# Two small edits in a fused two-layer transformer kernel: relative-bias rows from one 8-column matmul spread by the DMA, and indexer scores of an even and an odd head side by side

## The reference

```python
rel = jax.nn.relu(jnp.einsum("bqhd,bsd->bqhs", qib, k_idx_f))
score = jnp.einsum("bqhs,bqh->bqs", rel, wb) * idx_scale
score = jnp.where(admissible[None], score, -jnp.inf)
_, sel = lax.top_k(score, topk)
```

```python
dist = q_pos[:, None] - k_pos[None, :]
bias = jnp.transpose(rel_bias[rel_bucket(dist)], (2, 0, 1))
logits = jnp.einsum('bqhcd,bkhcd->bhcqk', q_blk, k) * scale + bias[None, :, None]
```

## Time and profile before

| | |
|---|---|
| median of 3 runs | 2699.56 us (2699.01 to 2699.8) |
| profiled execution, its own time | 2699.8 us |
| span of its profile | 2698.0 us |
| PE busy | 2584.3 us (96%) |
| DVE busy | 1684.5 us (62%) |
| ACT busy | 1286.2 us (48%) |
| granted clock of PE, mean | 0.988 |

### The profile page before, as it was taken

How to read it: one execution, slowest core, us unless ns; L and a number is a source line. 1 busy time by engine, 2 the same in 40 slices (tenths; PEclk the granted TensorE clock), 3 DMA queues, 4 the chain that set the end, 5 groups by cost and what they waited for, 6 DMA issues and landing times.

```text
span 2698.0 us, 28994 instructions
## 1 busy us (share of the span) xinstructions
PE 2584.3 (96%) x11660; PEld 2111.5 (78%) x11660; DVE 1684.5 (62%) x1914; ACT 1286.2 (48%) x1797; POOL 3.4 (0%) x10
## 2 busy tenths in 40 slices
PE   4999989999989999999999899999999999999998
PEld 3777767877868888888888787778788888888886
DVE  6899788988875555555555544666554454445455
ACT  4535666755454444444444454544454444444443
POOL 0000000000000000000000000000000000000000
PEclk9999999999989999999999999999999999999999
DMA  9888445777855556665554554345455555555553
GB/s 352 326 332 324 157 156 197 270 281 278 342 222 203 218 204 234 241 242 212 209 205 176 180 186 158 141 156 187 172 177 195 187 195 197 188 194 194 188 187 125
DMA packets 80566, 579.29 MB, mean 215 GB/s; under 512 B 8964, under 2 KB 8964, under 8 KB 10544
## 3 DMA queue, kind: packets, MB, share of 16 engines
q1 hardware_dynamic: 78480, 564.82, 57.8%
q10 hardware_dynamic: 1440, 9.81, 0.9%
q0 software_dynamic: 512, 2.81, 0.3%
HBM read 573.73 MB, written 3.67 MB: 214 GB/s over the span
## 4 chain that ended last, share of the span: by engine, by line
PE 76%; DVE 7%; ACT 3%; issue 1%; DMA 0%; ACTq 0%; DVEq 0%; SPq 0%
PE bank L640 72%; DVE wlo L1459 2%; PE bank L604 1%; ACT whi L965 1%; DVE raw L1469 1%; DVE X L1454 1%; DVE cv L1664 1%; ACT PR L965 0%; DVE SS L1454 0%; DVE cv L1454 0%; PE bank L752 0%; PE bank L800 0%; ACT SS L1335 0%; DMA raw<-in_w_in 0%; PE bank L885 0%
## 5 line engine op out<-in xcount | busy, mean ns | idle before, releaser
L1459 DVE TENSOR_TENSOR wlo<-raw,whi 128x1024 fp32r<-128x1024 f32 x882 | 1077.3, 1224 | 957.1 <-ACT whi L965 953.4
L965 ACT ACTIVATE whi<-raw 128x1024 fp32r<-128x1024 f32 x882 | 932.3, 1059 | 1289.2 <-PE bank L640 1169.2
L640 PE MATMUL bank<-whi,HTh 128*128 128x512 f32 x2560 | 706.2, 398 | 8.8 <-ACT HTh L965 5.8
L640 PE MATMUL bank<-wlo,HTh 128*128 128x512 f32 x2560 | 687.6, 391 | 3.5 <-DVE wlo L1459 3.5
L640 PE MATMUL bank<-whi,HTl 128*128 128x512 f32 x2560 | 689.2, 391 | 0.5 <-DVE HTl L1775 0.5
L640 PEld LDWEIGHTS bank<-wlo,HTh 128*128 128x128 f32 x2560 | 481.6, 188 | 106.4 <-DVE wlo L1459 4.8
L640 PEld LDWEIGHTS bank<-whi,HTl 128*128 128x128 f32 x2560 | 483.5, 189 | 103.7 <-DVE HTl L1775 1.0
L640 PEld LDWEIGHTS bank<-whi,HTh 128*128 128x128 f32 x2560 | 472.5, 189 | 113.9 <-issue 15.6
L1469 DVE CUSTOM_DVE_ANT_0 raw<-raw,GT,VECS 128x2048 f32<-128x2048 f32 x96 | 225.0, 2347 | 0.2 <-DMA raw<-in_w_ada 0.2
L640 PE MATMUL bank<-whi,ACTh 128*128 128x512 f32 x704 | 191.6, 394 | 0.0
L640 PE MATMUL bank<-wlo,ACTh 128*128 128x512 f32 x704 | 190.0, 392 | 0.0
(11 more groups left out here) (217 smaller groups left out, 1235.5 us busy)
## 6 DMA issues: line engine op xcount, KB each, us to landing
raw<-in_w_in SPq DMA_DIRECT2D x128, 1024.0 KB, 4.9
raw<-in_w_ada SPq DMA_DIRECT2D x96, 1024.0 KB, 6.5
raw<-in_w_gate SPq DMA_DIRECT2D x88, 1024.0 KB, 4.8
raw<-in_w_up SPq DMA_DIRECT2D x88, 1024.0 KB, 4.8
raw<-in_w_down SPq DMA_DIRECT2D x88, 1024.0 KB, 4.8
raw<-in_w_o SPq DMA_DIRECT2D x16, 1024.0 KB, 7.0
raw<-in_w_out SPq DMA_DIRECT2D x16, 1024.0 KB, 4.8
raw<-in_w_attn_out SPq DMA_DIRECT2D x8, 1024.0 KB, 4.8
```

The source lines that it names most:

```text
L640: i = e.matmul(bank[2 * ch.st + t][:, :], (xl if ps == 1 else xh)[:, k, tk(t)], (lo if ps == 2 else hi)[:, j * 512:j * 512 + 512], start=c ...
L965: return e.activation(dst, src, ACT.Copy, scale=scale)
L1459: e.tensor_tensor(lo, src, r32(hi), S_).then_inc(lo_done, 1)
```

## The change

Bias rows: one matmul with the eight heads as its eight columns gives all rows at once, in eight partitions; ACT copies them once; the scratch write repeats each row 128 times. The table `relb` is no longer repeated on the host. Scores: each slot takes an even and an odd head, which lie in the two halves of the array, for both halves of the tokens; the two heads go to banks 6 and 7, which are now one tensor `both`, and one ReLU reads 384 columns of each. The 384 are 256 of t = 1 and 128 of t = 0. Counters for the two halves become one.

```diff
-    RB = at("RB", 41984, [8, 128])
-    RD = at("RD", 50176, [8, 384])
+    RB = at("RB", 41984, [8])
+    RD = at("RD", 50176, [384])
...
+    rel = [at(f"rel{i}", 75776 + 4096 * i, [2, 512]) for i in range(2)]
...
-    bank = [nc.alloc_psum_tensor(f"bank{i}", [128, 512], f32) for i in range(8)]
+    bank = [nc.alloc_psum_tensor(f"bank{i}", [128, 512], f32) for i in range(6)]
+    both = nc.alloc_psum_tensor("bank67", [128, 2, 512], f32)
+    bank += [both[:, 0, :], both[:, 1, :]]
...
-            for h in R(8):
-                if h == 0:
-                    w.wait_ge(*xt_act(14))
-                else:
-                    w.wait_ge(*rb_act(h - 1))
-                e.matmul(bank[5][:, 0:384], RB[0:33, h, :], OH[0:33, :], start=True, stop=True).then_inc(*rb_pe.one(h))
-                yield 1
+            w.wait_ge(*xt_act(14))
+            e.matmul(bank[5][0:8, 0:384], RB[0:33, :], OH[0:33, :], start=True, stop=True).then_inc(*rb_pe.one("rows"))
+            yield 1
...
             for hp in R(8):
-                half = hp % 2
                 if hp:
-                    w.wait_ge(*sel_act[t](hp - 1))
-                for r in R(2):
-                    h = 4 * (hp // 2) + 2 * r + half
-                    i = e.matmul(b[:, r * 256:r * 256 + nk], qiT[64 * half:64 * half + 64, h // 2, tk(t)],
-                                 kiT[64 * half:64 * half + 64, 0:nk], start=True, stop=True)
-                i.then_inc(*sel_pe[t].one(hp))
+                    w.wait_ge(*sel_act(hp - 1))
+                for t in (1, 0):
+                    nk = 128 * (t + 1)
+                    for r in R(2):
+                        i = e.matmul(bank[6 + r][:, 256 - 256 * t:256 - 256 * t + nk], qiT[64 * r:64 * r + 64, hp, tk(t)],
+                                     kiT[64 * r:64 * r + 64, 0:nk], start=True, stop=True)
+                i.then_inc(*sel_pe.one(hp))
                 yield 1
...
-            for h in R(8):
-                w.wait_ge(*rb_pe(h))
-                copy(RD[:, h, :], bank[5][:, 0:384]).then_inc(*rb_act.one(h))
-                yield 1
+            w.wait_ge(*rb_pe("rows"))
+            copy(RD[0:8, :], bank[5][0:8, 0:384]).then_inc(*rb_act.one("rows"))
+            yield 1
...
-                e.activation(tri(sg[:, :], 2)[:, :, 0:nk], tri(b[:, :], 2)[:, :, 0:nk], ACT.Relu,
-                             scale=1.0 / 32).then_inc(*sel_act[t].one(hp))
+                e.activation(rel[hp % 2][:, :, 0:384], both[:, :, 0:384], ACT.Relu, scale=1.0 / 32).then_inc(
+                    *sel_act.one(hp))
...
                 for r in R(2):
-                    h = 4 * (hp // 2) + 2 * r + hp % 2
+                    sg = rel[hp % 2][:, r, 256 - 256 * t:256 - 256 * t + nk]
+                    h = 2 * hp + r
...
-        e.dma_start(A["scratch"], RD[:, :, :]).then_inc(scr_in, 16)
+        e.dma_start(A["scratch"].rearrange("p h i -> h p i"), RD[0:8, :].unsqueeze(1).to_broadcast([8, 128, 384])).then_inc(
+            scr_in, 16)
...
-    out["relb"] = np.broadcast_to(relb[:, :, None], (33, 8, 128))
+    out["relb"] = relb
```

More of the change, by code:

```diff
@@ L369, in build @@
     fh_act = steps("fh_act", list(R(16)))
-    rb_pe = steps("rb_pe", list(R(8)))
-    rb_act = steps("rb_act", list(R(8)))
+    rb_pe = steps("rb_pe", ["rows"])
+    rb_act = steps("rb_act", ["rows"])
     u_act = steps("u_act", [(j, t) for j in R(2) for t in R(2)])
@@ L377, in build @@
     two_dve = steps("two_dve", [0, 1])
-    sel_pe = [steps(f"sel{t}_pe", list(R(8))) for t in R(2)]
-    sel_act = [steps(f"sel{t}_act", list(R(8))) for t in R(2)]
+    sel_pe = steps("sel_pe", list(R(8)))
+    sel_act = steps("sel_act", list(R(8)))
     sel_dve = [steps(f"sel{t}_dve", [("s", hp, r) for hp in R(8) for r in R(2)] + ["outside"]
@@ L676, in bias_rows @@
             w.wait_ge(rb_in, 32)
-            for h in R(8):
-                if h == 0:
-                    w.wait_ge(*xt_act(14))
-                else:
-                    w.wait_ge(*rb_act(h - 1))
-                e.matmul(bank[5][:, 0:384], RB[0:33, h, :], OH[0:33, :], start=True, stop=True).then_inc(*rb_pe.one(h))
-                yield 1
+            w.wait_ge(*xt_act(14))
+            e.matmul(bank[5][0:8, 0:384], RB[0:33, :], OH[0:33, :], start=True, stop=True).then_inc(*rb_pe.one("rows"))
+            yield 1
         def t_job(n):
-            w.wait_ge(*rb_act(7))
+            w.wait_ge(*rb_act("rows"))
             if n:
@@ L700, in t_job, with select @@
             yield 1
-        def select(t):
-            nk = 128 * (t + 1)
-            b = bank[6 + (t == 0)]
+        def select():
             w.wait_ge(*tj_act("qi4", 1))
@@ L721, in attend @@
             bs = [bank[7]] if t == 0 else [bank[6], bank[5]]
-            w.wait_ge(*sel_act[t](7))
+            w.wait_ge(*sel_act(7))
             w.wait_ge(*tj_act("k4", 1))
@@ L936, in tensor @@
             lane.begin(TJ_SLOT[n], t_job(n))
+        lane.begin(SEL0, select())
         for t in R(2):
-            lane.begin(SEL0, select(t))
             lane.begin(ATT0 + 5 * (t == 0), attend(t))
@@ L1127, in t_job, with select @@
             yield 1
-        def select(t):
-            nk = 128 * (t + 1)
-            b = bank[6 + (t == 0)]
+        def select():
             for hp in R(8):
-                sg = stg[t + 2 * (hp % 2)]
-                w.wait_ge(*sel_pe[t](hp))
+                w.wait_ge(*sel_pe(hp))
                 if hp >= 2:
-                    w.wait_ge(*sel_dve[t]("s", hp - 2, 1))
-                e.activation(tri(sg[:, :], 2)[:, :, 0:nk], tri(b[:, :], 2)[:, :, 0:nk], ACT.Relu,
-                             scale=1.0 / 32).then_inc(*sel_act[t].one(hp))
+                    for t in R(2):
+                        w.wait_ge(*sel_dve[t]("s", hp - 2, 1))
+                e.activation(rel[hp % 2][:, :, 0:384], both[:, :, 0:384], ACT.Relu, scale=1.0 / 32).then_inc(
+                    *sel_act.one(hp))
                 yield 1
@@ L1168, in conv_products @@
             w.wait_ge(*cv_dve("pad"))
-            w.wait_ge(*rb_pe(7))
+            w.wait_ge(*rb_pe("rows"))
             w.wait_ge(*pro_dve("lam1"))
@@ L1588, in select @@
             for hp in R(8):
-                sg = stg[t + 2 * (hp % 2)]
-                w.wait_ge(*sel_act[t](hp))
+                w.wait_ge(*sel_act(hp))
                 for r in R(2):
-                    h = 4 * (hp // 2) + 2 * r + hp % 2
+                    sg = rel[hp % 2][:, r, 256 - 256 * t:256 - 256 * t + nk]
+                    h = 2 * hp + r
                     if prev is None:
-                        m = e.tensor_scalar(sc, sg[:, 0:nk], WI[:, t, 0:1], None, M_)
+                        m = e.tensor_scalar(sc, sg, WI[:, t, 0:1], None, M_)
                     else:
                         w.wait_ge(*sd(*prev))
-                        m = stt(sc, sg[:, r * 256:r * 256 + nk], WI[:, t, h:h + 1], sc, M_, A_)
+                        m = stt(sc, sg, WI[:, t, h:h + 1], sc, M_, A_)
                     m.then_inc(*sd.one("s", hp, r))
@@ L1989, in gpsimd @@
                         pattern=[[-1, 128]], channel_multiplier=1).then_inc(*pro_pool.one("ident"))
-        e.dma_start(RB[0:33, :, :], A["relb"]).then_inc(rb_in, 16)
+        e.dma_start(RB[0:33, :], A["relb"]).then_inc(rb_in, 16)
         e.dma_start(OH[0:33, :], A["onehot"]).then_inc(rb_in, 16)
-        w.wait_ge(*rb_act(7))
-        e.dma_start(A["scratch"], RD[:, :, :]).then_inc(scr_in, 16)
+        w.wait_ge(*rb_act("rows"))
+        e.dma_start(A["scratch"].rearrange("p h i -> h p i"), RD[0:8, :].unsqueeze(1).to_broadcast([8, 128, 384])).then_inc(
+            scr_in, 16)
         w.wait_ge(scr_in, 16)
```

## The result

The changed kernel takes 2709.68 us (median of 5 runs, 2708.52 to 2712.4); the kernel before took 2699.56 us beside it (2697.49 to 2700.39). The ratio is 1.0041, 95% interval 1.0026 to 1.0055: slower by about 10 us, against a forecast of 2692.0 with a range of 2688.5 to 2697.5. The profiled execution took 2708.52 us, with a span of 2706.7.

A forecast was written before the change was run, and what follows sets the result against it. PE, busy for 96% of the span, was taken as the bound, with DVE and the weight stream close in the first stage. Gains of 0.4 + 2.5 + 4.7 = 7.6 us gave 2692.0 us against the median of 2699.56, range 2688.5 to 2697.5.

The forecast's parts named there:

- the price of the scratch write: Scratch write in round 1: small rows cost no more per byte, 70 us of engine time; 8.7 us on eight engines.
- The term: Bias rows and scratch write, round 1 of the first stage: gain of 2.5 us, between 0.5 and 4.7.
- rival 4: Scratch write: small rows cost by the row, 170 ns each on eight engines, so slower, 2705 us; chance 0.05.
- My bound from the share of DMA: Round 1 of the first stage: 56.1 us of DMA time at a share of 0.95 takes 59.0 us.
- Rival 1: Scratch write on eight engines, or the denser stream, eats the whole bias-row gain; 2694.5 us; chance 0.25.
- Rival 2: Score slots: DVE becomes the bound, a third to a half of that gain stays there; 2694.2 us; chance 0.15.
- Rival 3: Whole change: everything comes through, 0.4 + 4.7 + 5.2 us, round 1 like its fastest sister; 2689 us; chance 0.07.
- The scores: Eight indexer slots: 0.65 us less in each, 5.2 us, with 0.5 off for DVE's waits: gain of 4.7 us.
- The start: Start of the kernel: bias table shrinks from 132 KB to 1 KB, gain of 0.4 us.
- Rounds 2 and 3: First stage, behind round 1: they might take back what it gave, since they share the stream; no size given.

The follow-up runs named there:

- e4_sixteen: The changed kernel with the eight rows held in all 128 partitions, each writing its row 8 times, scratch laid out by head; 2689.06 us, ratio 0.9959.
- e5_spread: The changed kernel with the eight rows in partitions 0, 4, ... 28 instead of 0 to 7; 2688.61 us, ratio 0.9966.
- e7_probe: The changed kernel with the scratch write held until piece 83 is done, plus six writes of 1.57 MB behind the last output store; executed once, 2807.92 us.
- e3_late: The changed kernel with the same scratch write issued only when piece 83 is done, in the score slots; 2687.44 us, ratio 0.9954.
- e1_scores: The kernel before with only the new scores, bias rows and scratch write as before; 2693.98 us, ratio 0.9981.
- e6_small: The changed kernel writing 16 copies of each row instead of 128, with BT loaded by eight transfers of 16 partitions; 2686.87 us, ratio 0.9961.
- e9_small_late: The changed kernel with 16 copies of each row, eight BT loads, and RB and OH loads held until four pieces are done; 2686.3 us, ratio 0.9958.

## Why the prediction was wrong, point by point

**The failed step: the price of the scratch write.** "So small rows cost no more per byte: 68 ns a row, 70 us of engine time", and "If eight partitions mean eight engines, those eight are busy for 8.7 us instead of 4.8". The rows per byte that I took were of transfers that read or write all 128 partitions. They were right as to bytes (61 and 64 us in `e4_sixteen` and `e5_spread`), and wrong for a source of eight neighbouring partitions: 185 us. With nothing beside it this write took 32.7 us in `e7_probe`, not 8.7, and in round 1 it held the weight stream down with it: 230 GB/s over 38 us in place of 324. The term was 2.5 us of gain; round 1 lost 14.6. Its range (0.5 to 4.7) had no mechanism in it that led below zero; only rival 4, with a chance of 0.05, had one.

**The gain that the term counted was there, and larger.** With the write out of the way round 1 takes 57.24 us, 6.5 less than before; with the write spread over all partitions 58.71, 5.0 less. My bound from the share of DMA (59.0 us at 0.95) was too cautious: `e4_sixteen` moves the same bytes at 0.92 in 58.71 us, its write at 61 us of engine time and not 76.7.

**Rival 1 (the write on eight engines eats the gain).** That eight partitions mean eight engines is borne out: 0.472 of 16 while nothing else ran. By itself that costs little: on eight engines, but spread (`e5_spread`), round 1 took 60.83 us, 2.1 more than in `e4_sixteen`, and still 2.9 less than before. The rule of the number of engines in the Trainium skill, "DMA: Bandwidth & Descriptors", section "Why a DMA increments its semaphore by 16 and not by 1", which the prediction set against the edit, agrees with `e7_probe` (half of the engines busy for eight rows, 0.94 for sixteen); what decided was the ports, of which the prediction says nothing. By the 435 GB/s that the Trainium skill, "SBUF — State Buffer", section "Door 1: The DMA port swizzle", gives for 16 ports, two carry 54, an estimate of 29 us for this write; 32.7 were measured in `e7_probe`.

**Rival 4 (slower, small rows by the row).** Its price of 170 ns a row and its time of 2705 us come near what was measured (185 us / 1024 = 181 ns; 2709.68), but not its cause: rows eight times as long take as long from the same partitions, and the same rows from partitions 0, 4, ... 28 take a third. Where the write runs alone it is 249 us of engine time (0.472 x 16 x 33), 243 ns a row, so that the price and the time came near is luck. The chance of 0.05 was too low, for "how it is spread over the engines no row shows" was an open question with no bound on it.

**Rival 2 (DVE binds in the score slots).** It did not come: 31.00 us against 30.8 forecast, DVE busy for 27.82 of it, and idle ahead of its split for 2.8 us, where I had written 1 (6.3 before). **Rival 3** was near in its terms: they are what `e3_late` does, at 2687.44 us.

**The scores.** Forecast 4.7 us; 5.1 between the same pieces, and 5.4 in the time of `e1_scores`. Slots start 3.82 us apart, and from the scores to the piece it is 0.85 us, as worked out from the logits. Halves of the array and banks of PSUM alternate together in the change. The starts of single matmuls in the traces tell them apart: in the slot before, where the bank changes but the half does not, the next matmul starts 0.11 us behind the last, as within a bank; with the change matmuls start in pairs 0.007 us apart, as in the logits before. So a change of bank alone gives nothing there; whether the halves would overlap within one bank no run shows. The timeline of PE after:

```profile
310.23 0.92 PE L711 MATMUL bank<-kiT,qiT 64*128 64x256 f32 x8
311.08 1.20 PE L643 MATMUL bank<-whi,HTh 128*128 128x512 f32 x4
...
314.05 0.92 PE L711 MATMUL bank<-kiT,qiT 64*128 64x256 f32 x8
314.90 1.20 PE L643 MATMUL bank<-whi,HTh 128*128 128x512 f32 x4
```

The joint ReLU costs 800 ns (0.83 forecast). The 0.5 us set aside for DVE's waits were not needed:

```profile
L1131 ACT ACTIVATE rel<-bank 128x768 f32<-128x768 f32 x8 | 6.4, 800 | 0.0
```

**The start.** Right in its direction, under its size: 0.4 us forecast from the bytes, 1.5 measured in the two profiles. The table's load is small, but it runs beside the loads that the first instructions wait for: ACT's first instruction on `GT` begins at 10.9 us with it (before, `e1_scores`) and at 8.9 to 10.0 in all other profiles. How it holds them up stays open.

**Rounds 2 and 3** took nothing back, as I had feared they might: 56.05 and 59.44 us.

The sum by its own terms, measured as gains: start 1.5, bias rows and write -14.6, scores 5.1, together -8.0 of the 8.7 us by which the span grew. With the write out of the way the bias rows gain 6.5, so the write's place and form cost 21.1 us.

## What to carry to other kernels

A transfer is priced by where it reads from as well as by its bytes: before data is made compact, ask how many partitions, and which, will feed the transfer, and how long that takes by itself; eight rows in partitions 0, 4, ... 28 went 3.6 times as fast as in 0 to 7. A slow transfer on a shared set of engines can cost the others far more than its bytes, so read it from more partitions, give it to a stage where the stream has slack, or make it smaller; the five versions that do one of these (`e3_late`, `e4_sixteen`, `e5_spread`, `e6_small`, `e9_small_late`) beat both kernels, at 0.9954 to 0.9966 of the time of before. And where a new form of a transfer has no row in the trace, the range must reach to what it would cost if it were bound by its source, not only by its bytes.

## What the runs showed of the hardware

- Rate of a write of 1.57 MB with nothing beside it: 48 GB/s from partitions 0 to 7, 91 from 0, 16, ... 112, 174 from 0, 4, ... 28, 99 from 0 to 15, 404 from all; the row length (1536 bytes or 12 KB) changed it from 48 to 51.
- Loads of 1 MB of weights beside such a write land after 20 to 26 us, though they are on another queue; beside the spread or the small write they take 7 to 11 (`e5_spread`, `e6_small`). The whole rate fell to 230 GB/s over 38 us, where 324 had been moved in the same stretch before. That the engines which hold the slow packets serve the other queue late is what the busy shares suggest; it was not measured apart from a contention at the source.
- Fp32 matmuls of 64 rows that alternate between the halves of the array and two banks start in pairs 0.007 us apart; a slot's four take 0.85 us, where the same four from one half took 1.50.
